# A one-core hybrid decoder step on Trainium2: part of the chunk loop's element work put on GpSimd, and four small reorderings

## What is computed

```python
acs = jnp.cumsum(dtc * a, axis=2)
decay = jnp.exp(jnp.where(causal, acs[l] - acs[s], -jnp.inf))
scores = jnp.einsum('bclgn,bcsgn->bclsg', cc, bc)
wgt = scores[..., None] * decay * dtc[:, :, None]
y_diag = jnp.einsum('bclsgk,bcsgkp->bclgkp', wgt, xc)
states = jnp.einsum('bclgn,bclgk,bclgkp->bcgkpn', bc, decay_end, xc)
h = h * chunk_decay + states            # one chunk after the other
y_off = jnp.einsum('bclgn,bcgkpn,bclgk->bclgkp', cc, h_prev, jnp.exp(acs))
y = y_diag + y_off + xs * d_skip        # the skip term
y = rmsnorm(y * silu(z), ssm_norm)      # the gate, then the norm over 768 channels
out = concatenate([pool_out, y]) @ w_out
```

## Time and profile before

| | us |
|---|---|
| device time, median of 3 runs | 2202.85 (2201.61 to 2203.3) |
| the profiled execution | 2200.24 |
| its span, first to last instruction | 2198.2 |
| TensorE busy | 2176.1 (99%) |
| VectorE busy | 1378.6 (63%) |
| ScalarE busy | 703.5 (32%) |
| GpSimd busy | 329.9 (15%) |
| mean granted TensorE clock | 0.997 |

### The profile page before, as it was taken

The page is one execution under the profiler, slowest core; times in us unless marked ns, Lnnn a source line. Parts: engine busy times, 40 slices in busy tenths (PEclk is TensorE's granted clock), DMA queues, the critical chain, the costliest instruction groups (busy, mean ns, idle before and its releaser), DMA issues.

```text
span 2198.2 us, 40671 instructions
## 1 busy us (share of the span) xinstructions
PE 2176.1 (99%) x15886; PEld 2126.6 (97%) x15886; DVE 1378.6 (63%) x2528; ACT 703.5 (32%) x1143; POOL 329.9 (15%) x334
## 2 busy tenths in 40 slices
PE   8999999999999999999999999999999999999998
PEld 8999999999999999987899998999999999999998
DVE  6865655546667675456877456268755555466665
ACT  6332232222113332245724145133322222221124
POOL 2010110113322000023400001000110010133230
PEclk9999999999999999999999999999999999999999
DMA  7232231253323221138733334441222132153222
GB/s 237 67 109 63 63 111 58 67 185 115 105 89 104 86 55 42 36 119 270 230 102 124 134 116 154 145 129 40 83 91 82 58 100 74 60 210 117 78 78 79
DMA packets 222576, 234.36 MB, mean 107 GB/s; under 512 B 8979, under 2 KB 179745, under 8 KB 222201
## 3 DMA queue, kind: packets, MB, share of 16 engines
q1 hardware_dynamic: 222465, 232.83, 32.5%
HBM read 180.42 MB, written 52.48 MB: 106 GB/s over the span
## 4 chain that ended last, share of the span: by engine, by line
PE 62%; DVE 2%; ACT 1%; issue 0%; DMA 0%; SPq 0%; DVEq 0%; ACTq 0%
PE bank L3130 19%; PE bank L3132 18%; PE bank L3131 18%; PE bank L3847 1%; PE bank L3690 0%; PE bank L3953 0%; PE bank L3686 0%; PE bank L3857 0%; PE bank L3869 0%; PE bank L3696 0%; DMA out_mem_k_prompt_dram<-kst 0%; PE bank L3825 0%; PE bank L3541 0%; PE bank L3709 0%; PE bank L3612 0%
## 5 line engine op out<-in xcount | busy, mean ns | idle before, releaser
L3130 PE MATMUL bank<-h_hi,w_hi 128*128 128x352 f32 (+1 forms) x3392 | 1048.6, 309 | 0.3
L3131 PE MATMUL bank<-h_lo,w_hi 128*128 128x352 f32 (+1 forms) x3392 | 1040.1, 307 | 0.0
L3132 PE MATMUL bank<-h_hi,w_lo 128*128 128x352 f32 (+1 forms) x3392 | 1040.0, 307 | 0.0
L3130 PEld LDWEIGHTS bank<-h_hi,w_hi 128*128 128x128 f32 x3392 | 637.0, 188 | 2.3 <-issue 0.7
L3131 PEld LDWEIGHTS bank<-h_lo,w_hi 128*128 128x128 f32 x3392 | 637.9, 188 | 0.0
L3132 PEld LDWEIGHTS bank<-h_hi,w_lo 128*128 128x128 f32 x3392 | 636.8, 188 | 0.0
L2272 DVE SCALAR_TENSOR_TENSOR x<-bank,x 128x352 f32<-128x352 f32 x448 | 226.8, 520 | 129.6 <-PE bank L3132 128.9
L3131 PE MATMUL bank<-xr,w_hi 128*128 128x264 f32 x640 | 181.8, 284 | 0.0
L3130 PE MATMUL bank<-xr,w_hi 128*128 128x264 f32 x640 | 181.4, 284 | 0.1
L3132 PE MATMUL bank<-xr,w_lo 128*128 128x264 f32 x640 | 181.5, 284 | 0.0
L1058 POOL TENSOR_TENSOR act<-p,act 128x264 f32<-128x264 f32 x40 | 38.2, 955 | 812.5 <-DVE p L2145 812.5
(11 more groups left out here) (450 smaller groups left out, 2935.6 us busy)
## 6 DMA issues: line engine op xcount, KB each, us to landing
act_keep<-act SPq DMA_DIRECT2D x88, 264.0 KB, 2.0
w_raw<-in_w_gate_dram SPq DMA_DIRECT2D x44, 512.0 KB, 5.0
w_raw<-in_w_up_dram SPq DMA_DIRECT2D x44, 512.0 KB, 3.9
w_raw<-in_w_down_dram SPq DMA_DIRECT2D x44, 512.0 KB, 3.6
h_raw<-act_keep SPq DMA_DIRECT2D x24, 528.0 KB, 4.6
l_raw<-act_keep SPq DMA_DIRECT2D x20, 528.0 KB, 5.3
w_raw<-in_w_in_dram SPq DMA_DIRECT2D x18, 512.0 KB, 4.3
x<-x_keep SPq DMA_DIRECT2D x6, 1408.0 KB, 9.7
```

Of the source, the lines that this page charges most:

```text
L3130: eng.matmul(out, a_hi, b_hi, start=first, stop=False, skip_group_check=onto)
L3131: eng.matmul(out, a_hi, b_lo, start=False, stop=False, skip_group_check=onto)
L3132: return eng.matmul(out, a_lo, b_hi, start=False, stop=last, skip_group_check=onto)
```

## The change

- The store `kv_out(0)` is issued ahead of `kv_unit(7)`, two weight units earlier.
- `scale_c` on VectorE keeps the first head group only. The second group's product is a new GpSimd step, `scale_end`, right behind `end_weight`; TensorE waits for it by `g_done` before head 6 of the state part.
- The skip term of head pairs 4 and 5 leaves TensorE. GpSimd computes d_skip times x times z for these pairs (`skip_gated`, two instructions of 256 elements, into the last third of `dsk`) before `gate_chunk` overwrites `xs`, and adds it after the gate (`add_skip`, one of 256). `gate_chunk` waits for the first, `y_square` for the second. `dsk` on TensorE is filled for four pairs only.
- `chunk_y` takes the four remaining skip products first and waits for `h_upd` before head 8.
- TensorE no longer waits for the mask of chunk 2 (`sm_done`) before `chunk_state(1)`.
- ScalarE waits for the last chunk's y where it waited for its state before `pool_hi(0)` and `y_square(8)`.
- The `ffn_add` of tiles 0 and 1 are put between the steps of `newton` in `y_scale(0)`.

```diff
             for j in range(4, 12):
+                if j == 7:
+                    kv_out(0)
                 kv_unit(j)
...
-                if j == 8:
-                    kv_out(0)
                     kt_out(0)
...
-                wait(eng, c_ready, 2 * (q_ - 1))
+                wait(eng, c_ready, q_ - 1)
...
+            def scale_end(q_):
+
+                eng.wait_ge(s_x[3], 32 + 16 * (q_ - 1))
+                c3 = cea[q_ % 2][:, HG:HEADS, :]
+                eng.tensor_tensor(c3, c3, bc(bcT[:, 3, (q_ - 1) * P:q_ * P].unsqueeze(1), [P, HG, P]), ALU.mult)\
+                   .then_inc(g_done, 1)
+
+            def skip_gated(q_):
+
+                tok = chunk(q_)[2]
+                link(eng.tensor_tensor(dsk[:, 4:6, :], xs[:, 4:6, tok], bc(dskip[:, 4:6].unsqueeze(2), [P, 2, P]), ALU.mult))
+                eng.tensor_tensor(dsk[:, 4:6, :], dsk[:, 4:6, :], z[:, 4:6, tok], ALU.mult).then_inc(g_done, 1)
+
+            def add_skip(q_):
+
+                tok = chunk(q_)[2]
+                eng.wait_ge(y_ev, q_ + 1)
+                eng.wait_ge(g_done, skipped(q_))
+                eng.tensor_tensor(xs[:, 4:6, tok], xs[:, 4:6, tok], dsk[:, 4:6, :], ALU.add).then_inc(g_done, 1)
+                if q_ < CH:
+                    eng.wait_ge(g_done, skip_added(q_))
+                    skip_gated(q_ + 1)
+
             out_low(0)
             end_weight(1)
+            skip_gated(1)
             out_low(1)
...
             end_weight(2)
+            scale_end(2)
             for q_ in range(2, CH + 1):
                 eng.wait_ge(h_upd, q_ - 1)
...
+                add_skip(q_ - 1)
                 if q_ < CH:
                     end_weight(q_ + 1)
+                    scale_end(q_ + 1)
+            add_skip(CH)
             add_squares(CH - 1)
             add_squares(CH)
...
-                    eng.wait_ge(g_done, 1)
+                    eng.wait_ge(y_ev, 1)
+                    eng.wait_ge(g_done, 2)
+                else:
+                    eng.wait_ge(g_done, skip_added(q_))
                 eng.activation(z[:, :, tok], xs[:, :, tok], ACT.Square).then_inc(r_sq, 1)
...
                 eng.wait_ge(yd_ready, q_ + 1)
+                eng.wait_ge(g_done, skipped(q_))
                 eng.tensor_tensor(xs[:, 0:4, tok], a[:, :].rearrange("p (j l) -> p j l", j=4), z[:, 0:4, tok], ALU.mult)
...
-            y_scale(0)
+            y_scale(0, lambda step: ffn_add(1, LAST, 2, step))
...
+                for j in range(YT):
+                    o = a[:, P * j:P * j + P] if j < 4 else b[:, P * (j - 4):P * (j - 4) + P]
+                    outs += [o[0:HD], o[HD:P]]
+                    if j < 4:
+                        eng.matmul(o, dsk[:, j, :], xs[:, j, tok], start=j == 0, stop=False)
+                for h in range(HEADS):
+                    if h % HG == 0:
+                        eng.wait_ge(wg_ready, 2 * q_ + h // HG + 1)
+                    if h == 8:
                         wait(eng, h_upd, q_ - 1)
...
+                        if h == HG:
+                            eng.wait_ge(g_done, 3 * q_ - 3)
                         mm = eng.matmul(outs[h], hT[:, HD * h:HD * h + HD], cea[q_ % 2][:, h, :], start=False, stop=h in ends)
...
                 chunk_y(q_)
-                eng.wait_ge(sm_done, min(q_ + 2, CH + 1))
                 if q_ >= 2:
+                    eng.wait_ge(sm_done, min(q_ + 2, CH + 1))
                     partial_sums(q_ - 2)
```

More of the change, by code:

```diff
@@ L461, in unit_at, with skipped, skip_added @@
             return u // MH, HEADS_AT[u % MH]
+        def skipped(q):
+            return 3 * q - 1 if q > 1 else 1
+        def skip_added(q):
+            return 3 * q + 1 if q < CH else 3 * q
         def squared(q):
@@ L1909, in link, with newton @@
                 return ins
-            def newton(ms, y, s):
+            def newton(ms, y, s, between=None):
                 link(eng.tensor_scalar(y.bitcast(I32), ms.bitcast(I32), 1, None, ALU.logical_shift_right))
@@ L1919, in newton @@
                     link(eng.scalar_tensor_tensor(out=y, in0=s, scalar=1.5, in1=y, op0=ALU.add, op1=ALU.mult))
+                    if between and step < 2:
+                        between(step)
             def norm_sum(v, n):
@@ L2641, in scale_c @@
                 eng.wait_ge(s_x[3], 32 + 16 * (q_ - 1))
[L2642 to L2645, removed]
+                c3 = cea[q_ % 2][:, 0:HG, :]
+                eng.tensor_tensor(c3, c3, bc(bcT[:, 2, (q_ - 1) * P:q_ * P].unsqueeze(1), [P, HG, P]), ALU.mult)\
+                   .then_inc(c_ready, 1)
             def gate_chunk(q_):
@@ L3084, in y_sums, with y_scale @@
                 eng.tensor_tensor(sqs[:, cols(n)], sq[:, 0, :], sq[:, 1, :], ALU.add).then_inc(n_sum, 1)
-            def y_scale(group):
+            def y_scale(group, between=None):
                 t = slice(0, 5) if group == 0 else slice(5, 9)
@@ L3092, in y_scale @@
                 eng.sem_inc(n_ms, 1)
-                newton(nrm[:, 0, t], nrm[:, 1, t], nrm[:, 2, t])
+                newton(nrm[:, 0, t], nrm[:, 1, t], nrm[:, 2, t], between)
                 eng.sem_inc(n_rs, 1)
@@ L3104, in _ @@
                     y_sums(1)
-            y_scale(0)
+            y_scale(0, lambda step: ffn_add(1, LAST, 2, step))
             y_out(0)
             y_out(1)
-            for m in range(KT + 1):
+            for m in range(2, KT + 1):
                 if m < KT:
@@ L3679, in chunk_y @@
                 outs, ends = [], (6, 7, 10, 11)
[L3680 to L3691 removed]
+                for j in range(YT):
[7 more added lines that the diff above has]
+                    if h == 8:
+                        wait(eng, h_upd, q_ - 1)
+                    mm = eng.matmul(outs[h], xdt[q_ % 2][:, h, :], dec[(q_ - 1) % 3][:, h, :], start=h in (8, 9),
+                                    stop=q_ == 1 and h in ends)
                 if q_ > 1:
                     for h in range(HEADS):
[L3694 to L3695 removed]
+                        if h == 0:
+                            eng.wait_ge(c_ready, q_ - 1)
+                        if h == HG:
+                            eng.wait_ge(g_done, 3 * q_ - 3)
                         mm = eng.matmul(outs[h], hT[:, HD * h:HD * h + HD], cea[q_ % 2][:, h, :], start=False, stop=h in ends)
@@ L3726, in chunk_sums @@
                 if q_ > CH - 2:
-                    eng.wait_ge(g_done, 1 + q_ - (CH - 2))
+                    eng.wait_ge(g_done, 3 * CH + 1 + q_ - (CH - 1))
                     sums = z[:, 0, tok]
```

21 lines of the change are left out of this document (4 added, 17 removed).

## The result

The changed kernel takes 2212.36 us (median of 6 executions, 2211.53 to 2214.29), the kernel before in the same comparison 2201.40 (6 executions, 2200.91 to 2203.30). The ratio is 1.0048, 95% interval 1.0038 to 1.0059. It is slower by 11.0 us, where +13.2 was forecast; the time of 2212.4 lies inside the range of 2206 to 2222. The time forecast, 2216.0, is 3.6 too high: 2.2 of that is the difference, and 1.4 is the kernel before, whose median is 2201.40 in this comparison and was 2202.85 in the runs that the forecast was added to.

The account below looks back on a forecast made before the run. GpSimd, sharing a port with VectorE, was to bound the chunk loop: 13.4 + 1.0 - 0.95 - 0.25 = +13.2 us on the profiled 2200.24 gives 2213.4, plus 2.6 for the median 2216.0; range 2206 to 2222.

Parts of the forecast that it names:

- The bound and the sign: Chunk loop: GpSimd with the shared port sets the round; hc should follow hc at 9.1 to 9.3 us.
- Rival C: Chunk loop: new GpSimd work is hidden and TensorE stays the bound; 8 x 0.64 = 5.1 us saved, 2196 us; chance 0.09.
- Rival B: Chunk loop: half the port's cost falls into existing waits; round about 8.2 us, 2203 to 2210 us; chance 0.10.
- Part 2: Chunk loop: GpSimd's own work per chunk rises to 6.73 us from 2.94, with scale_end taken as 1.79.
- Part 3: Chunk loop: three VectorE products each hold the port 0.81 us, so GpSimd's round is 6.73 + 3 x 0.81 = 9.16 us.
- Part 4, the ends: Whole chunk loop, first and last chunks included: the last update ends at 1110.75 instead of 1097.37, +13.4 us.
- Part 4, the first projection: After the loop: VectorE's splits of x take turns with GpSimd's adding of squares, +1.0 us.
- Part 1: Chunk loop: removing two skip products saves TensorE 0.64 us per chunk, period 8.06 to 7.42, busy time some 5 us less.
- Part 5: Remaining small edits: mask wait 0, key store -0.95, last rows -0.25, ScalarE's reordering and y_square's new wait 0 us.
- Key store: Keys, ahead of the loop: with the store issued earlier, TensorE goes on at 994.1 instead of 995.07, -0.95 us.
- Mask wait: At chunk_state(1): TensorE's 1.19 us wait goes, but the step also waits for the last sample state, so 0.
- Last rows: Kernel's end: moving two adds ahead of the row factors wins only VectorE's wait for TensorE at 2183.49, -0.25 us.

Follow-up runs that it names:

- e4: Changed kernel with GpSimd's new products replaced by fills of about the same total length, waits kept, output not the reference's: 2204.20 us, kernel before 2202.28.
- e3: Changed kernel with both C products back on VectorE, skip term of pairs 4 and 5 still on GpSimd: 2209.17 us, kernel before 2202.28.
- e5: Changed kernel with only pair 5's skip term on GpSimd (three instructions of 128 elements), pair 4 back on TensorE: 2206.46 us, kernel before 2201.94.
- e1: Kernel before plus only the small edits (key store, mask wait, ScalarE's order, row factors), nothing moved to GpSimd: 2200.95 us, kernel before 2202.28.
- e6: Changed kernel with the skip of pairs 4 and 5 added by VectorE in PSUM instead of GpSimd, scale_end still on GpSimd: 2202.17 us, kernel before 2201.94.
- e7: As e6, but VectorE adds the skip of pairs 2 to 5 in PSUM: 2202.19 us, kernel before 2201.94.
- e8: As e6, but both C products on VectorE, so nothing new on GpSimd: 2200.88 us, kernel before 2201.94.
- e9: As e6, but VectorE's two weight splits moved from ahead of chunk 8's gate to behind the last state update: 2200.10 us, kernel before 2201.55.

## Why the prediction was right, and where it was off

- **The bound and the sign.** The forecast that GpSimd with the port sets the round held: no idle time of GpSimd in the round, all three VectorE products inside it, the 256-element instructions stretched to 1.21 to 1.45, TensorE waiting for `hT` before head 8 six times. The round of 8.73 lies below the 9.1 to 9.3 that was named as its sign. Rival C's condition (the products do not hold the port) is refuted by the 3.44 of `weigh`, and e4, where the new instructions meet it, took 2204.20 and not C's 2196. Rival B gave the round that e3 has, not that of the change.
- **Part 2, GpSimd's own work: right.** The round of 8.73, less the three turns below (1.97), leaves 6.76; the forecast was 6.73. `scale_end` has 1.79 from start to start, as taken.
- **Part 3, the turn: mis-sized.** 0.81 for each, from the one meeting of the earlier trace rows that showed a stall alone. Undisturbed, at the end of the changed kernel, the rows are:

```profile
1105.87 0.61 POOL L1184 TENSOR_TENSOR dsk<-xs,dskip 128x256 f32<-128x256 f32 x1
1106.56 0.73 POOL L1185 TENSOR_TENSOR dsk<-dsk,z 128x256 f32<-128x256 f32 x1
...
1108.50 0.73 POOL L1192 TENSOR_TENSOR xs<-xs,dsk 128x256 f32<-128x256 f32 x1 [1.20 <-DVE xs L2694]
```

  From start to next start each is 0.69 (1105.87 to 1106.56, 1108.50 to 1109.19), and `add_skip` has a self-wait of 0.07 behind it in the loop. Taken from the spacings of 1.54, 1.28 and 1.29 that leaves 0.78, 0.59 and 0.60. The first turn is nearly as forecast, the second and third are 0.2 shorter: 1.97 instead of 2.43. e5 has the same pattern (0.76, 0.59, 0.59). Both shorter ones are turns of a VectorE product that stood behind another waiting VectorE product. That some of its start-up is over by the time it gets its turn would fit, but no run shows it.
- **Part 4, the ends: near in each place, the sum too large mainly by five rounds of 0.43.** On the time base of before (0.94 taken off, the start's 1.9 less the keys' 0.96) `hc(2)` began at 1048.2 (forecast 1048.75), `hc(3)` at 1057.1 (1057.2), `hc(7)` at 1092.0 (1093.8), the last update ended at 1108.4 (1110.75). `weigh(1)` was late as worked out: its pair took 3.77 behind GpSimd's split. So the last update comes 11.0 later on that base, forecast 13.4; of the 11.0, 0.3 arose ahead of TensorE's first skip product and 10.7 in the loop.
- **Part 4, the first projection: the size right, the cause wrong.** From the last update on the projection is 1.1 us longer, forecast +1.0 for VectorE's splits of x beside GpSimd's squares. TensorE has no wait there that could come of it. It runs slow instead, windows view of the changed kernel:

```profile
1108.00:1110.00 2.00, 0.59 (x3) 0.60 (x4) 1.97 (x5) 0.73 (x1) 1.50 (x2) 0.81 1.17 325
1110.00:1112.00 2.00, 1.86 (x8) 1.49 (x7) 2.00 (x3) 2.00 (x6) 1.84 (x4) 0.50 0.68 165
1112.00:1114.00 2.00, 2.00 (x13) 2.00 (x12) 2.00 (x3) 2.00 (x6) 1.84 (x3) 0.83 0.00 0
```

  0.67 on the transposes (1.54 for 0.87) and five products 0.13 further apart make 1.3, which covers the 1.1. The idle TensorE at the end of the loop was part of the forecast; that its clock would answer was not. That +1.0 and +1.1 agree is luck.
- **Part 1: short of the mark in two ways.** Without a wait the new period is 7.26 (e4), not 7.42: 0.80 saved a chunk, not 0.64. In the changed kernel that was worth nothing, as said. And the busy time did not fall by 5 us but by 0.8 in all and 2.9 in the loop (59.82 to 56.90, in the 62.2 and 72.9 us above): a round with waits in it has 7.82 us of recorded busy time, e4's without them 7.26 for the same matmuls. Recorded busy time of TensorE was no measure of the work removed here.
- **Part 5.** Key store -0.96 (forecast -0.95). Mask wait 0 in the change, as forecast, for the reason given (the sample state, 1.85). Last rows about -0.55, forecast -0.25, as more of the two adds fell into the gaps of the factor chain than was counted. e1 gives the small edits together -1.3 [-4.0, 0.0 by its interval], forecast -1.2 without the mask wait. ScalarE's `y_square` behind `add_skip` was put at 0; TensorE stood 4.1 us behind it, each time with a wait for `hT` to follow, so no time is seen from it.
- **The sum.** 10.7 + 1.1 - 0.96 - 0.55 = +10.3, and with the 0.3 between the keys and the loop +10.6, which is the 12.5 between the spans less the 1.9 ahead of 990 us. (e1 has 0.4 between keys and loop as well; no run shows why.) Between the medians it is 11.0. The forecast's +13.2 was too high by 2.2, and five rounds of 0.43 too much make 2.2.

What the prediction did not see at all is that C would have been wrong even without the port: e4 is that case, and is not below the kernel before. It gave the hidden GpSimd work -5.1 us by TensorE's shorter period. e6, e7 and e8 have nearly that period without the skip on GpSimd, and the best of them, e8, gains 1.1, no more than the small edits alone in e1 (1.3). VectorE, with 1.2 us of slack a round, was the next bound, 0.6 below what the first had been (7.41 and 7.35 for 8.06), and the first and last chunks had each their own chain.

## What to carry to other kernels

Before moving element work to GpSimd, count how many VectorE instructions with two SBUF inputs fall between its own: each costs GpSimd a turn (0.6 to 0.8 us here for 768 elements) however short its instruction is, so that many short products on GpSimd cost far more than their own lengths. A removed piece of the leading engine is worth no more than the slack of the second in the steady rounds, and may be worth nothing in the first and last ones, where other chains end last: work out the first round, the steady one and the end each by itself. A VectorE instruction with an input in PSUM took no turn here (the gate kept its 0.69 beside `end_weight`'s 1.47), but it still needs time on VectorE, and e6 and e7 had none to spare.

## What the runs showed of the hardware

- GpSimd fills do not take turns with VectorE's two-input products: 0.31 us for 256 elements beside an undisturbed `scale_c` of 0.95, and 0.74 for 768 (at 1047.10) beside a `weigh` pair of 1.83 (e4). The `hc` of the same kernel, which reads, does: 2.17 instead of 1.47.
- Turns that follow one another are cheaper for GpSimd than a single one: 0.78, then 0.59 and 0.60 (changed kernel), 0.76, 0.59 and 0.59 (e5).
- TensorE's granted clock fell to 0.50 for some microseconds at the end of the loop in six of the kernels: after waits of 2.18 and 2.13 close together (the change), 1.14 and 2.12 (e3), 1.20 and 2.10 (e4), 1.55 and 1.64 (e5), or one of 2.8 (e6, e7). In e4 it also fell in chunk 2, behind a single wait of 2.28, where the changed kernel kept 1.00 behind its 2.31. It did not fall in e9, with four waits of 0.40 to 0.99 in 6 us. So the length of a wait alone does not decide; what does is left open. The price in e6, on transposes and 15 products, was 2.7 us (0.67 and 15 times some 0.135).
